# Two query units of a sliding-window mixer: eight half products each, or seven products of sums of halves

## The reference, cut to what matters

```python
def mixer_c(hn, w_in, b_in, sinks, w_out, b_out, cos, sin):
    B, S, _ = hn.shape
    proj = hn @ w_in + b_in
    q, k, v = jnp.split(proj, [W_Q_SWA, W_Q_SWA + W_KV_SWA], axis=-1)
    q = apply_rope(q.reshape(B, S, N_HEADS_SWA, HEAD_DIM), cos, sin)
    k = apply_rope(k.reshape(B, S, N_KV_SWA, HEAD_DIM), cos, sin)
    v = v.reshape(B, S, N_KV_SWA, HEAD_DIM)
    o = sliding_window_gqa_sinks(q, k, v, sinks)
    return o.reshape(B, S, W_Q_SWA) @ w_out + b_out
```

## Time and profile before

| | before |
|---|---|
| median of 3 runs | 1136.28 us (1134.83 to 1136.38) |
| the profiled execution's own time | 1134.69 us |
| its span | 1132.8 us |
| PE busy | 828.3 us (73%) |
| PE weight loads | 434.9 us (38%) |
| DVE busy | 159.4 us (14%) |
| ACT busy | 156.4 us (14%) |
| POOL busy | 67.1 us (6%) |
| DMA | 438.31 MB, mean 387 GB/s |

### The profile page before, as it was taken

One profiled execution on the slowest core, in us unless ns is written; L12 is line 12 of the kernel. 1 busy time (PEld: TensorE's weight loads), 2 busy tenths in 40 slices (PEclk: granted clock), 3 DMA queues, 4 the chain that ended last, 5 costly groups with the idle time before them and its releaser, 6 DMA issues.

```text
span 1132.8 us, 13387 instructions
## 1 busy us (share of the span) xinstructions
PE 828.3 (73%) x5754; PEld 434.9 (38%) x5754; DVE 159.4 (14%) x427; ACT 156.4 (14%) x346; POOL 67.1 (6%) x88
## 2 busy tenths in 40 slices
PE   9999999835666374738779999965647365755876
PEld 8685684301313131304444576331313113221524
DVE  1143442000000000000014535100000000000002
ACT  2246231000000000000020444100000000000102
POOL 0010020000000000000001552000000000000000
PEclk9999999977879697878999999976888778787988
DMA  9942669999999999999999647999999999999995
GB/s 382 419 186 111 267 275 382 429 448 426 433 424 436 431 438 420 436 440 433 420 418 426 255 178 318 427 428 444 440 418 424 448 431 422 426 446 433 426 427 205
DMA packets 22543, 438.31 MB, mean 387 GB/s; under 512 B 2528, under 2 KB 3552, under 8 KB 7008
## 3 DMA queue, kind: packets, MB, share of 16 engines
q1 hardware_dynamic: 21232, 434.39, 90.4%
q10 hardware_dynamic: 1264, 3.23, 0.7%
HBM read 436.56 MB, written 1.05 MB: 386 GB/s over the span
## 4 chain that ended last, share of the span: by engine, by line
DMA 54%; PE 41%; DVE 2%; ACT 1%; issue 1%; POOL 1%; SPq 0%; DVEq 0%; ACTq 0%; POOLq 0%
DMA store<-in_w_down 21%; DMA store<-in_w_gate 18%; PE bank L1261 16%; DMA store<-in_w_up 14%; PE bank L962 5%; PE bank L1004 5%; PE bank L1104 4%; PE bank L1399 1%; PE bank L941 1%; PE bank L970 1%; PE bank L1205 1%; PE bank L1194 1%; PE bank L1284 1%; PE bank L1039 0%; PE bank L1017 0%
## 5 line engine op out<-in xcount | busy, mean ns | idle before, releaser
L1261 PE MATMUL bank<-store,hg 128*32 128x512 f32 x2048 | 281.8, 707 | 221.7 <-DMA store<-in_w_up 113.2
L1261 PEld LDWEIGHTS bank<-store,hg 128*32 128x32 f32 x2048 | 72.5, 127 | 414.0 <-issue 264.8
L1261 PE MATMUL bank<-store 128*32 128x512 f32 x880 | 112.1, 658 | 59.6 <-DMA store<-in_w_down 58.2
L1261 PEld LDWEIGHTS bank<-store 128*32 128x32 f32 x880 | 32.5, 120 | 131.5 <-issue 129.7
L1780 DVE TENSOR_TENSOR store<-store,bank 128x512 f32<-128x512 f32 x16 | 11.0, 688 | 491.3 <-PE bank L1261 491.3
L962 PE MATMUL bank<-store,hg 128*128 128x512 f32 x160 | 71.2, 596 | 0.0
L1104 PE MATMUL bank<-store 128*128 128x256 f32 x256 | 64.5, 389 | 0.0
L1004 PE MATMUL bank<-hg,store 128*128 128x256 f32 x256 | 58.0, 387 | 1.3 <-DMA store<-w_ab 1.3
L1194 PEld LDWEIGHTS bank<-store,hr 128*128 128x128 f32 x448 | 51.5, 193 | 12.8 <-issue 12.8
L1194 PE MATMUL bank<-store,hr 128*128 128x128 f32 x448 | 54.1, 279 | 0.0
L645 POOL TENSOR_TENSOR store<-store,gate_all 128x256 f32<-128x256 f32 x16 | 9.8, 615 | 738.8 <-PE bank L941 720.9
(11 more groups left out here) (213 smaller groups left out, 589.5 us busy)
## 6 DMA issues: line engine op xcount, KB each, us to landing
store<-in_w_up SPq DMA_DIRECT2D x12, 4096.0 KB, 25.4
store<-in_w_down SPq DMA_DIRECT2D x20, 2048.0 KB, 24.7
store<-in_w_up SPq DMA_DIRECT2D x16, 2048.0 KB, 16.2
store<-in_w_gate SPq DMA_DIRECT2D x16, 2048.0 KB, 12.4
store<-in_w_down SPq DMA_DIRECT2D x6, 4096.0 KB, 23.8
store<-in_w_down SPq DMA_DIRECT2D x14, 1024.0 KB, 27.8
store<-w_ab SPq DMA_DIRECT2D x6, 2048.0 KB, 30.6
store<-wo_ab SPq DMA_DIRECT2D x2, 2048.0 KB, 27.7
```

The costliest lines, as they stand in the source:

```text
L1261: op = pe.matmul(dst[rows, :], lhsT[:, q, rows], moving, start=(q == 0), stop=(q == steps - 1))
```

## The change

For units 1 and 2 the 256 x 1024 state and the 1024 x 512 weights are each cut into 2 x 2 quarters (token blocks by even or odd row chunks; row chunks by left or right 256 columns). A block product of such quarters takes eight products of quarters, which is what the 16 matmuls of 128x512 do. The change forms it from **seven** products of sums and differences of quarters. Each product is 4 matmuls of 128x256.

- DVE forms four combinations of the state once (`sum_x`, 4 operations of 128x512) and, for each unit, four combinations of the weights (`mix_right`, `mix_left`, `mix_used`, each one operation of 128x1024; three of them overwrite the weights in their slot).
- Three of the four output quarters are prefixes of one running sum in a PSUM bank, so ACT copies that bank out, times rstd, before PE may add the next product (`keep`, three times, then `keep_last`). The kept parts lie in `c_q` (`c_raw`). DVE adds the other products to them (`whole_first`, one operation, `whole_rest`, three). `add_bias` for units 1 and 2 then adds the bias to the finished raw queries.
- In the hand-written order of PE, unit 2's products 1 to 3 stand ahead of `turn_q(0)`, product 4 ahead of the first scores, product 5 behind them, products 6 and 7 behind the second scores. The third scores go between `turn_p(0)` and `turn_p(1)`. DVE does `inverse(1)` before `copy_odd(0)`.
- ACT waits for `cc["roped"]` at 2 before the first `keep` of unit 2.

The core of the diff:

```diff
+            def keep(u, dst, part):
+                l = u // AB_UNITS
+                b, cols = ((0, LO), (0, HI), (1, HI))[part]
+                act.wait_ge(sevens["product"], PRODUCTS * SEVENS.index(u) + (1, 3, 5)[part])
+                act.activation(dst[:, b, cols], bank[SEVEN_BANKS[u][0]][:, LO], ACT.Copy,
+                               scale=rstd[:, 2 * l, b:b + 1]).then_inc(sevens["kept"], 1)
...
+            act.wait_ge(rooted, 3)
+            for part in range(KEPT):
+                keep(C_LOW, c_raw(C_LOW), part)
+            keep_last(C_LOW, c_raw(C_LOW), cc["used"], 2)
             turn_in(cc["k_turned"], 1, c_kT, (6, 7), 1.0, cc["k"])
+            act.wait_ge(cc["roped"], 2)
+            keep(C_HIGH, c_raw(C_HIGH), 0)
+            keep(C_HIGH, c_raw(C_HIGH), 1)
             turn_in(cc["q_turned"], 1, c_qT[0], (4, 5), -(HD ** -0.5), cc["q"])
...
+            def product(dst, x, w, start=False):
+                for k in range(4):
+                    op = pe.matmul(dst, x[:, k, :], w[:, k, :], start=(start and k == 0), stop=(k == 3),
+                                   skip_group_check=True)
+                return op
...
+                product(sums[:, LO], x_quarter(l, 0, 0), w_quarter(u, 0, 0), start=True).then_inc(sevens["product"], 1)
+                product(pair[:, LO], x_quarter(l, 0, 1), w_quarter(u, 1, 0), start=True).then_inc(sevens["product"], 1)
+                pe.wait_ge(sevens["w_turned"], TURNS * at + 1)
+                pe.wait_ge(sevens["kept"], KEPT * at + 1)
+                product(sums[:, LO], rest, w_mixed[u]).then_inc(sevens["product"], 1)
...
-            project(bank[2:4], slot_in(c_slot(1)), chunks=C_CHUNKS).then_inc(cc["used"], 1)
+            seven_products(C_LOW, cc["used"])
...
-            high_q(0, 6)
+            three_products(C_HIGH)
             turn_q(0)
-            high_q(6, 8)
+            fourth_product(C_HIGH)
             swa_scores(0)
-            high_q(8, 12)
+            fifth_product(C_HIGH)
             swa_scores(1)
-            high_q(12, 14)
+            last_products(C_HIGH, cc["used"])
             turn_p(0)
-            high_q(14, 15)
+            swa_scores(2)
             turn_p(1)
-            high_q(15, 16).then_inc(cc["used"], 1)
-            swa_scores(2)
             swa_values(0)
...
+            def mix_used(u):
+                at = SEVENS.index(u)
+                dve.wait_ge(sevens["w_turned"], TURNS * at + 1)
+                dve.wait_ge(sevens["product"], PRODUCTS * at + 1)
+                dve.tensor_tensor(w_quarter(u, 0, 0), w_quarter(u, 1, 1), w_mixed[u], ALU.subtract).then_inc(sevens["w_turned"], 1)
+                dve.wait_ge(sevens["product"], PRODUCTS * at + 2)
+                dve.tensor_tensor(w_quarter(u, 1, 0), w_quarter(u, 1, 0), w_mixed[u], ALU.subtract).then_inc(sevens["w_turned"], 1)
...
-            for u in range(2):
-                add_bias(u)
-                add_swapped(u)
+            add_bias(0)
+            add_swapped(0)
+            mix_used(C_LOW)
+            dve.wait_ge(w_landed[AB_UNITS - RING + 2], 32)
+            mix_right(C_HIGH)
+            dve.wait_ge(sevens["product"], PRODUCTS * SEVENS.index(C_LOW) + 3)
+            mix_left(C_HIGH)
+            whole_first(C_LOW, c_raw(C_LOW))
+            whole_rest(C_LOW, c_raw(C_LOW))
+            add_bias(1)
+            add_swapped(1)
+            mix_used(C_HIGH)
```

More of the change, by code:

```diff
@@ L35 @@
 C_CHUNKS = [0, 2, 4, 6, 1, 3, 5, 7]
+C_LOW, C_HIGH = AB_UNITS + 1, AB_UNITS + 2
 EXPERTS = 32
@@ L238, in hybrid_trunk @@
         c_bin, c_kT = carve(C_IN * HALF), carve(KV_HEADS, S)
+        c_x_all, c_x_rest, c_x_high = (carve(4, P) for _ in range(3))
         assert pos[0] <= spare(1) + UNIT
@@ L319, in hybrid_trunk @@
         out_done = sem("out_done")
+        sevens = {n: sem("sevens_" + n) for n in ("w_turned", "product", "kept", "kept_last", "whole")}
         ab = {n: sem("ab_" + n) for n in (
@@ L451, in hr_bank, with x_quarter, c_raw, w_quarter @@
             return bank[(7, 4)[b] if high else 4 + b]
+        SEVENS = (C_LOW, C_HIGH)
+        SEVEN_BANKS = {C_LOW: (2, 3, 4), C_HIGH: (0, 1, 2)}
+        PRODUCTS, TURNS, KEPT = 6, 3, 3
+        LO, HI = slice(0, S), slice(S, HALF)
+        def x_quarter(l, b, high):
+            chunks = slice(high, KD, 2) if l else slice(4 * high, 4 * high + 4)
+            return hg[:, chunks, b * P:(b + 1) * P]
+        def c_raw(u):
+            return c_q[:, :, (u - C_LOW) * HALF:(u - C_LOW + 1) * HALF]
+        def w_quarter(u, high, right):
+            unit = slot_in(u % RING if u < AB_UNITS else c_slot(u - AB_UNITS))
+            return unit[:, 4 * high:4 * high + 4, HI if right else LO]
         def head_rows(t, head, chunk=None):
@@ L751, in blocks, with keep_last @@
                 return [t[:, b, :] for b in range(NB)]
+            def keep(u, dst, part):
[4 more added lines that the diff above has]
+                               scale=rstd[:, 2 * l, b:b + 1]).then_inc(sevens["kept"], 1)
+            def keep_last(u, dst, done, count):
+                l = u // AB_UNITS
+                act.wait_ge(done, count)
+                act.activation(dst[:, 1, LO], bank[SEVEN_BANKS[u][0]][:, LO], ACT.Copy,
+                               scale=rstd[:, 2 * l, 1:2]).then_inc(sevens["kept_last"], 1)
             def log1p(g):
@@ L912, in _ @@
             probs(0)
+            keep(C_HIGH, c_raw(C_HIGH), 2)
             probs(1)
+            keep_last(C_HIGH, c_raw(C_HIGH), cc["used"], 3)
             copy_even(0)
@@ L1564, in _, with sum_x @@
             mean_out(0, bank[4])
+            def sum_x(l):
+                whole, rest, high, apart = x_sums[l]
+                dve.wait_ge(scaled, SCALED[2] + len(ACT_CHUNKS) if l else KD)
+                dve.tensor_tensor(apart, x_quarter(l, 0, 0), x_quarter(l, 1, 0), ALU.subtract)
+                link(dve.tensor_tensor(whole, x_quarter(l, 1, 0), x_quarter(l, 1, 1), ALU.add))
+                link(dve.tensor_tensor(rest, whole, x_quarter(l, 0, 0), ALU.subtract))
+                dve.tensor_tensor(high, x_quarter(l, 0, 1), rest, ALU.subtract)
@@ new lines, in add_kept, with whole_first @@
+            def add_kept(u, out, src, b):
+                return dve.scalar_tensor_tensor(out=out, in0=src, scalar=rstd[:, 2 * (u // AB_UNITS), b:b + 1], in1=out,
+                                                op0=ALU.mult, op1=ALU.add)
+            def whole_first(u, dst):
+                at = SEVENS.index(u)
+                dve.wait_ge(sevens["product"], PRODUCTS * at + 4)
+                dve.wait_ge(sevens["kept"], KEPT * at + 1)
+                add_kept(u, dst[:, 0, LO], bank[SEVEN_BANKS[u][1]][:, LO], 0)
@@ new lines, in whole_rest @@
+            def whole_rest(u, dst):
+                at = SEVENS.index(u)
+                across, high = bank[SEVEN_BANKS[u][2]][:, LO], bank[SEVEN_BANKS[u][1]][:, HI]
+                dve.wait_ge(sevens["product"], PRODUCTS * at + 6)
+                dve.wait_ge(sevens["kept"], KEPT * at + 3)
+                add_kept(u, dst[:, 0, HI], across, 0).then_inc(dve_step, 1)
+                steps[0] += 1
+                add_kept(u, dst[:, 1, HI], across, 1)
+                dve.wait_ge(dve_step, steps[0])
+                add_kept(u, dst[:, 0, HI], high, 0).then_inc(sevens["whole"], 1)
@@ L1831, in _ @@
             op.then_inc(summed, 1)
+            sum_x(1)
             mean_out(2, bank[5])
+            dve.wait_ge(w_landed[AB_UNITS - RING + 1], 32)
+            mix_right(C_LOW)
+            mix_left(C_LOW)
             dve.wait_ge(rows_in, 32)
```

60 lines of the change are left out of this document (51 added, 9 removed).

## The result

The changed kernel took 1138.76 us as the median of 8 executions (1136.64 to 1139.66), the kernel before 1135.57 us beside it (8 executions, 1133.70 to 1136.38). The ratio is 1.003 with a 95% interval of 1.002 to 1.004: **slower**, by about 3.2 us (0.3%), clear of the noise. The forecast of 1135.4 us and its range, which ended at 1137.7, both miss. The profiled execution took 1138.61 us, its span is 1136.8 us.

The account below looks back on a forecast made before the run. PE was taken to bound the second mixer, with the experts' weight stream starting at its end. Terms -1.65 + 0.35 + 0.45 = -0.85 us against the median 1136.28 gave 1135.4 us; range 1133.7 to 1137.7.

Parts of the forecast that it names:

- Unit 1, -1.65: PE's products of unit 1: 56 records in 12.1 us instead of 13.75, ending at 618.3 instead of 619.96; -1.65 us.
- To the second rotation, -1.3 in all: From unit 1's end to the second rotation: `keep_last` and bias from SBUF add +0.35 us, so -1.3 us remain.
- The added wait: PE stands 2.6 us before unit 2's product 3, awaiting `keep`; +0.45 us, leaving a gain of 0.85 us.
- From there to the first values, 0: PE from the low queries' transposes to the first values: open copy offset by vanished waits; 0, bounds -0.7 and +0.74.
- Later pairs untouched, 0 to +0.3: Behind the first values: high queries' bias ends just when PE asks, PE full in later pairs; bounds 0 and +0.3.
- Rival 1, the clock: PE's idle 2.6 us before product 3 lowers its clock: +1.7 us, 1137.1 us, slower than before; chance 0.37.
- Rival 2, no stall, -3.0 us: ACT gives unit 2's first `keep` right behind product 1, so PE does not stand: -3.0 us, 1133.3; chance 0.08.
- Rival 3, late mixes: DVE's four mixes per unit take 2.5 us each, delaying unit 1's products 6 and 7; with clock drop +2.35, 1138.6; chance 0.04.
- Rival 4, nothing moves: The mixer's end is not the start of the experts' weight stream, so time stays 1136.3 us; chance 0.04.

Follow-up runs that it names:

- second profile: The changed kernel run once more, unaltered: median 1138.51 us, ratio 1.003 to the kernel before; its profiled execution took 1135.93 us.
- Unit 1 alone: The changed kernel with unit 2 and the order of the first pairs put back as before the change: 1134.08 us, ratio 0.9989 to the kernel before.
- The split: The changed kernel without ACT's wait for the rotation, DVE's cosines and swapped addition of the high queries moved behind `inverse(2)`: 1133.32 us, ratio 0.9983.
- first profile: The changed kernel's first measurement, nothing altered: median 1138.76 us, ratio 1.003 to the kernel before; its profiled execution took 1138.61 us.
- the early keep: The changed kernel without ACT's wait for the second rotation ahead of unit 2's first `keep`: 1134.03 us, ratio 0.9992 to the kernel before.
- the two reorderings: Changed kernel, cosines behind `inverse(2)`, products 6 and 7 around `turn_p`; also without ACT's rotation wait: 1132.31 us, ratio 0.9973 to the kernel before.

## Why the prediction was wrong

By its steps, in mixer times and with the execution that kept its clock (second profile), so that the clock stands apart:

- **Unit 1, -1.65.** Right: 56 records in 12.10 us without a gap, all mixes and sums under cover, the transposes of the keys at 26.34 instead of 27.99.
- **To the second rotation, -1.3 in all.** Right: it ends at 33.20 (predicted 33.16). Unit 1 alone brought -1.26 us to the end.
- **The added wait.** The mechanism was right and PE stood 3.01 us, not 2.6: PE arrived earlier, because eight transposes occupy it for 0.87 us, not 1.09, which costs nothing; and `keep` took 0.47 us, not the 0.384 that I took from L903, a copy of the same size without the scale per token that `keep` reads. The transposes of the low queries come at 35.65, where product 3's predicted start (33.66) and eight records give 35.4. Off by 0.2 to 0.3 us.
- **From there to the first values, 0.** This step failed. Both ends of the leg give 48.14 - 34.51 = 13.63 us before, and 48.10 - 33.85 = 14.25 now: **+0.62 us**, near the upper bound of 0.74. The open copy came; the waits of before that I let go against it were 0.20 us in all in this leg, which explains 0.74 - 0.20 = 0.54 of the 0.62. I had the row for the new wait and no row for the old ones, and the lower bound of -0.7 had none either.
- **Later pairs untouched, 0 to +0.3.** This step failed too: **+1.04 us**, of which the gaps of 0.57 and 0.30 us are 0.87. I checked when the bias of the high queries *ends*, and not what runs beside it and stands behind it. Taking it from SBUF (1.61 us with POOL's scaling beside it) and having POOL free earlier brought cosines and sines together; the masks and `copy_odd(1)` are queued behind. The price stood in the trace of before, in the sines of the low queries (3.45 us in the earlier trace rows). The split gave 0.79 us of it back.
- **The sum without a fall of the clock** was therefore -0.66 + 0.62 + 1.04 = +1.0 us instead of -0.85. The fall adds 1.59 and is the largest single term: the sum had it at nothing, as a rival. Together they make the +2.59 of the first profile.
- **Rival 1, the clock.** Price right (+1.7 predicted; 1.56, 1.59 and 1.67 measured), chance too low: I called it a toss at 0.37, and by the times of the changed kernel it seems to be the rule. The four gaps from which I took the odds, two each way, all stand in the experts' stages, in front of matmuls of other shapes; what makes the clock fall behind one gap and not behind the next is not shown. The Trainium skill (TensorE: Matmul & The Clock Gate, "Why this matters for your kernels") advises against idle gaps of about this length; I had read it as making the predicted 2.6 us harmless. The trace agrees in two gaps of 3.01 and 3.02 us, and not in two others of the same length.
- **Rival 2, no stall, -3.0 us.** Its start was right: without the wait product 3 runs in the latency and the transposes come at 33.25. But the -3.0 us needed the rest of the leg to be free. Alone the early keep gives -1.28; with the two reorderings -2.70, and the median -3.11. The rival's number belongs to that kernel.
- **Rival 3, late mixes:** no; the pairs of mixes took 1.2 us each and held nobody up. **Rival 4, nothing moves:** no; the table above shows the time moving with the mixer almost one to one.

The range was too narrow at the top because its upper end held the clock's fall on top of a sum without the two failed steps. The clock and the failed steps are independent, and they came together. Against before, the forecast was -0.85 us and the medians give +3.19. Of these 3.19 us, 2.59 are shown in the first profile; the rest, 0.6 us, lies inside the interval (2.3 to 4.5 us) and I have no row for it. Not tried: an early keep together with product 4 ahead of the transposes, which would fill the 0.70 us that PE still waits there.

## What to carry to other kernels

Work that is saved on an engine which is filling someone else's latency is worth nothing until the latency is shortened too: say what the engine does in the time that comes free. If a hand-written order leaves it standing, fill the stall with useful work, or as here with idle matmuls, since the slow clock behind it can cost more than the change gains: 1.6 us here, against 1.26 from unit 1. And where a change moves an operation earlier, write down for each of its new neighbours what is queued behind it and what runs beside it on the other engine: here two such places (a copy with nothing left to cover it, cosines beside sines) cost 1.3 to 1.4 us by the kernels that take them out, slightly more than the 1.26 that unit 1 brought.

## What the runs showed of the hardware

- The granted clock behind gaps of the same length is not the same each time: behind 3.01 and 3.02 us it fell to 0.50 in two profiles and stayed 1.00 in two. In one of the last two it fell behind a later gap of 2.55 us. A fall behind the stall costs 1.56 to 1.67 us here. With idle matmuls up to 0.57 us before the wait's end it stayed 1.00 in both profiles.
- DVE's multiplication of two SBUF inputs (two of 128x512) takes 1.26 to 1.29 us beside POOL's scaling and 2.37 beside POOL's multiplication; POOL's multiplication takes 2.48 to 2.50 beside DVE's masks and 3.44 beside DVE's multiplication. A small operation of DVE on two SBUF inputs (128x4, 0.16 us elsewhere) takes up to 1.09 beside POOL's multiplication. POOL's scaling (four of 128x128) takes 2.98 to 3.00 us beside DVE's masks, and up to 4.62 beside two pairs of DVE's operations of 128x512 on two SBUF inputs.
- ACT's copy of 128x256 out of PSUM takes 0.47 us with a scale from a tile, 0.38 to 0.39 without.
